# Feed-forwards on tokens and context: output pairs as seven half-size products, the second product in six parts

## The reference

```python
def swiglu(h, w1, w2):
    a, b = jnp.split(h @ w1, 2, axis=-1)
    return (jax.nn.silu(a) * b) @ w2

def ffn_sublayer(x, m, i, g, w1, w2):
    return x + HALF_STEP * m[:, 3 * i + 2, None] * swiglu(mod_norm(x, m, i, g), w1, w2)
# in second_block, for each layer l
m = (jax.nn.silu(c) @ w_mod[l] + b_mod[l]).reshape(B, N_MOD, D_MODEL)
x = ffn_sublayer(x, m, 0, norm_g[l, 0], ffn_w_in[l, 0], ffn_w_out[l, 0])      # "a"
xc = ffn_sublayer(xc, mc, 0, norm_g[l, 0], ffn_w_in[l, 0], ffn_w_out[l, 0])
...                                                                          # mixers, attention
x = ffn_sublayer(x, m, 2, norm_g[l, 2], ffn_w_in[l, 1], ffn_w_out[l, 1])      # "b"
```

## Time and profile before

| | |
|---|---|
| median of 3 runs | 3590.39 us (3589.85 to 3597.12) |
| the profiled execution | 3599.08 us |
| its span, first to last instruction | 3597.2 us |
| TensorE matmul, weight load busy | 95%, 81% |
| VectorE, ScalarE, GpSimd busy | 52%, 32%, 8% |
| mean granted TensorE clock | 0.974 |

### The profile page before, as it was taken

One profiled execution on the slowest core, in us unless ns is written; L12 is line 12 of the kernel. 1 busy time (PEld: TensorE's weight loads), 2 busy tenths in 40 slices (PEclk: granted clock), 3 DMA queues, 4 the chain that ended last, 5 costly groups with the idle time before them and its releaser, 6 DMA issues.

```text
span 3597.2 us, 45611 instructions
## 1 busy us (share of the span) xinstructions
PE 3413.5 (95%) x18534; PEld 2913.1 (81%) x18534; DVE 1884.1 (52%) x3688; ACT 1156.6 (32%) x1892; POOL 274.7 (8%) x520
## 2 busy tenths in 40 slices
PE   6989889998999999999789999999999999889998
PEld 5788667886888888878678888888888888778886
DVE  5476668446655535465677775352222364653333
ACT  4465442324221223334432122242112243332232
POOL 0000011000111100301011110000000013100000
PEclk9999899999999999999999999999999999989999
DMA  4301236333444423523145553232222244123332
GB/s 125 91 24 42 76 119 194 97 94 101 142 124 129 126 68 120 150 79 89 36 149 158 161 163 109 81 102 64 65 65 60 76 132 107 43 65 97 93 99 76
DMA packets 383473, 358.83 MB, mean 100 GB/s; under 512 B 19632, under 2 KB 351280, under 8 KB 382880
## 3 DMA queue, kind: packets, MB, share of 16 engines
q1 hardware_dynamic: 350656, 261.76, 24.1%
q0 software_dynamic: 31168, 91.94, 8.5%
q10 hardware_dynamic: 1440, 2.22, 0.2%
HBM read 349.56 MB, written 2.10 MB: 98 GB/s over the span
## 4 chain that ended last, share of the span: by engine, by line
PE 83%; DVE 11%; ACT 4%; issue 1%; DMA 1%; ACTq 0%; DVEq 0%; POOLq 0%
PE ps L626 81%; DVE lob L1964 2%; PE ps L629 1%; DVE Tm L2076 1%; ACT hib L1324 1%; DVE Hl L2087 1%; DVE ACC L2053 1%; ACT Tm L1324 1%; ACT Hh L1324 1%; DVE sm L2665 1%; ACT L1324 0%; DVE HN L2096 0%; DVE MR L1984 0%; DVE near_P L2675 0%; DVE Hl L2085 0%
## 5 line engine op out<-in xcount | busy, mean ns | idle before, releaser
L626 PE MATMUL ps<-Hh,hib 128*128 128x512 f32 (+1 forms) x3584 | 1271.0, 355 | 29.8 <-DVE lob L1964 13.4
L626 PE MATMUL ps<-Hl,hib 128*128 128x512 f32 (+1 forms) x3584 | 1260.7, 352 | 0.0
L626 PE MATMUL ps<-Hh,lob 128*128 128x512 f32 (+1 forms) x3584 | 1258.3, 351 | 0.0
L1964 DVE TENSOR_TENSOR lob<-rawb,hib 128x1024 fp32r<-128x1024 f32 (+2 forms) x499 | 597.4, 1200 | 983.6 <-ACT hib L1324 982.9
L1324 ACT ACTIVATE hib<-rawb 128x1024 fp32r<-128x1024 f32 (+2 forms) x499 | 513.6, 1033 | 1156.6 <-PE ps L626 1135.6
L626 PEld LDWEIGHTS ps<-Hh,hib 128*128 128x128 f32 x3584 | 685.1, 191 | 138.3 <-DVE lob L1964 15.3
L626 PEld LDWEIGHTS ps<-Hh,lob 128*128 128x128 f32 x3584 | 685.1, 191 | 90.1
L626 PEld LDWEIGHTS ps<-Hl,hib 128*128 128x128 f32 x3584 | 686.1, 191 | 86.6 <-issue 1.2
L626 PE MATMUL ps<-Gha,hib 128*128 128x512 f32 (+1 forms) x704 | 239.7, 340 | 6.6 <-DVE lob L1964 6.5
L626 PE MATMUL ps<-Gla,hib 128*128 128x512 f32 (+1 forms) x704 | 238.1, 338 | 0.0
L626 PE MATMUL ps<-Gha,lob 128*128 128x512 f32 (+1 forms) x704 | 238.1, 338 | 0.0
(11 more groups left out here) (264 smaller groups left out, 3807.8 us busy)
## 6 DMA issues: line engine op xcount, KB each, us to landing
rawb<-in_ffn_w_in SPq DMA_DIRECT2D x352, 256.0 KB, 3.3
rawb<-in_ffn_w_out SPq DMA_DIRECT2D x88, 512.0 KB, 3.4
rawb<-in_w_in SPq DMA_DIRECT2D x74, 512.0 KB, 3.8
MRb<-in_w_mod_t POOLq DMA_DIRECT2D x144, 256.0 KB, 3.4
rawb<-in_w_ff SPq DMA_DIRECT2D x64, 512.0 KB, 3.6
MRa<-in_w_mod_t POOLq DMA_DIRECT2D x96, 256.0 KB, 3.4
rawb<-in_ffn_w_out SPq DMA_DIRECT2D x44, 384.0 KB, 3.0
rawb<-in_w_out SPq DMA_DIRECT2D x28, 512.0 KB, 3.4
```

The lines of the kernel that those rows point to most:

```text
L626: return e.matmul(out, lhsT, rhs, start=start, stop=stop)
L1964: e.tensor_tensor(lob_of(c), raw_of(c), hib_of(c), ALU.subtract).then_inc(*done(("lo", c.i)))
```

## The change

In a0, b0 and a1 the parts of the feed-forward are 2, 4, 4, 4, 4 and 4 output pairs instead of 11 and 11 (b1 stays as it is). The first two pairs of a stage are computed as before; the other 20 by Strassen's scheme: the weights of a pair are a 2 x 2 matrix of blocks (even and odd k-tiles; gate and value columns), the activations one too (even and odd k-tiles; tokens 0 to 383 and 384 to 767), and seven products of sums of blocks take the place of eight. A product (`seven`) is 4 k-tiles x 3 matmuls of 384 columns into a PSUM bank of its own.

- GpSimd makes the five sums of weight blocks of each pair (`weights_sums`: two in place in `rawb`, three in `SUM2`), a step of 128 x 512 each. ScalarE and VectorE make high and low halves of all seven as units of 512 columns; `hib` and `lob` become a ring of six such units.
- The sums of activation blocks are made once a stage, 20 steps of 384 columns of each kind, in groups beside the two plain pairs and the first part's sweep: VectorE adds the high halves and subtracts the rounded sum, ScalarE rounds, GpSimd adds the low halves, and GpSimd (12) or VectorE (8) adds both rests.
- ScalarE copies three of the seven products out of PSUM, VectorE combines them in eight adds, then silu, multiply, high and low half on 384 columns, twice.
- The rows of `w_mod`: 48, 96, 48 and 96 in the first block, a0, b0 and a1. ScalarE's queue issues their loads in place of GpSimd's, at its next step, when VectorE has used a slot. In a crossed pair two rows are made (b0: one), in a chunk of the sweeps of parts 1 to 4 three (b0: two); what is left is made before the last sweep.

```diff
+ORDER = [1, 7, 6, 5, 3, 4, 2]
+ACTS = {1: (1, 1, 4), 7: (2, -1, 4), 6: (3, -1, 1), 5: (1, 1, 2), 2: (3, 1, 4), 3: (1,), 4: (4,)}
+WEIGHTS = {1: (1, 1, 4), 7: (3, 1, 4), 6: (1, 1, 2), 3: (2, -1, 4), 4: (3, -1, 1), 5: (4,), 2: (1,)}
+SUMS = [(m, q) for m in (1, 7, 6, 5, 2) for q in range(4)]
+SUMS_BY = (4, 4, 4, 2, 2, 2, 2)
+PLAIN = 2
+HALF = 384
+TURNS = {("a", 0): 1, ("b", 0): 2, ("a", 1): 3}
+def parts_of(j, l):
+    sizes = (PLAIN, 4, 4, 4, 4, 4) if crossed(j, l) else (11, 11)
...
-        mod_turns = [(0, 0, 48, 2), (0, 48, 96, 2), (1, 0, 144, 3)]
+        mod_turns = [(0, 0, 48, 2, 0), (0, 48, 96, 3, 2), (1, 0, 48, 2, 1), (1, 48, 96, 3, 2)]
...
# TensorE
+            def seven(N, name):
+                for x in P[name].units:
+                    b, before = take("o", name, x.m)
+                    w.wait_ge(*at("lo", x.u))
+                    freed(before)
+                    for q in range(4):
+                        if len(ACTS[x.m]) == 3:
+                            w.wait_ge(*at("e", N, x.m, q))
+                        wh, wl = (half_of(buffer, x)[:, 128 * q:128 * q + 128] for buffer in (hib, lob))
+                        mm(ps[:, b, 0:HALF], wh, acts_sum(N, 0, x.m, q), q == 0, False)
+                        mm(ps[:, b, 0:HALF], wh, acts_sum(N, 1, x.m, q), False, False)
+                        m = mm(ps[:, b, 0:HALF], wl, acts_sum(N, 0, x.m, q), False, q == 3)
+                    m.then_inc(*done(("full", name, x.m), ("used", x.u)))
...
-                    ga = {s: (Gh, Gl, OFF[s][0], OFF[s][1], (lambda k, s=s: ("g", (j, l), part_, s, k)), False) for s in sets}
+                    ga = {s: (Gh, Gl, OFF[s][0], OFF[s][1], (lambda k: ("g", N, part_, k)), False) for s in sets}
...
# ScalarE
+            def mod_more():
+                while mod["owed"] and mod["at"] < many:
+                    w.wait_ge(*at("modused", turn, u - 3 if u >= 3 else None))
+                    e.dma_start(mod_slots[turn][m], ...)
...
+                for pos, x in enumerate(P[name].units):
+                    mod_more()
+                    high_halves(reach(u=x.u))
+                    run_later()
+                    if mod["turn"] is not None and pos in (2, 4) and pos // 2 <= mod_turns[mod["turn"]][4]:
+                        mod_used(1)
+                    if pos == 6:
+                        gate("a1")
+                        high("a1", 0)
+                        gate("a2")
+                        high("a2", 1)
+                    elif x.m in copied:
+                        copy(copied[x.m], x.m)
...
# VectorE
+                for pos, x in enumerate(P[name].units):
+                    low_halves(reach(u=x.u))
+                    run_later()
+                    if m == 1:
+                        tmp("seven", name, "b2")
+                    elif m == 7:
+                        w.wait_ge(*at("copied", name, "b2"))
+                        add("a1", slot("b2"), product(7), ALU.add, ("free", "o", name, 7))
+                    elif m == 6:
+                        add("b2", slot("b2"), product(6), ALU.add, ("free", "o", name, 6))
+                    elif m == 5:
+                        w.wait_ge(*at("copied", name, "b1"))
+                        own()
+                        add("a1", slot("a1"), slot("b1"), ALU.subtract)
+                    elif m == 3:
+                        own()
+                        add("b1", slot("b1"), product(3), ALU.add)
+                        add("b2", slot("b2"), product(3), ALU.add, ("free", "o", name, 3))
+                    elif m == 4:
+                        w.wait_ge(*at("copied", name, "a2"))
+                        own()
+                        add("a1", slot("a1"), slot("a2"), ALU.add, ("whole", name, "a1"))
+                    else:
+                        gated("a1", "b1")
+                        add("a2", slot("a2"), product(2), ALU.add, ("whole", name, "a2"))
+                        add("b2", slot("b2"), product(2), ALU.subtract, ("free", "o", name, 2))
+                        low("a1", 0)
+                        own()
+                        gated("a2", "b2")
+                        low("a2", 1, ("g", N, part, f))
+                    if mod["turn"] is not None and pos in (2, 4):
+                        mod_step(1 if pos // 2 <= mod_turns[mod["turn"]][4] else 0)
...
# GpSimd
+            def weights_sums(N, name, before):
+                for c in x.chunks:
+                    w.wait_ge(*at("raw", c.i))
+                for m in (1, 7, 6, 3, 4):
+                    b1, sign, b2 = WEIGHTS[m]
+                    if m in (1, 7, 6):
+                        w.wait_ge(*at("lo", before[m] if before else None))
+                    else:
+                        own()
+                    e.tensor_tensor(weights_source(N, of[m]), weights_block(x, b1), weights_block(x, b2),
+                                    ALU.add if sign > 0 else ALU.subtract).then_inc(*done(("sum", of[m].u)))
```

More of the change, by code:

```diff
@@ new lines, in ffn @@
+                for part_, (f0, many) in enumerate(parts):
+                    for f in range(f0, f0 + many):
+                        name = (N, "in", f)
+                        if crossed(*N) and f >= PLAIN:
+                            seven(N, name)
+                        else:
+                            whole(name, fm_products, acts, between)
+                            between = None
+                            give_all(name)
+                            mark("pe", "plain", N)
+                    ga = {s: (Gh, Gl, OFF[s][0], OFF[s][1], (lambda k: ("g", N, part_, k)), False) for s in sets}
+                    residual((N, "out", part_), sets, ga, following(l, i) if part_ == len(parts) - 1 and len(sets) == 2 else None)
+                    mark("pe", "gfree", N, part_)
@@ L1367, in gemm @@
-            def gemm(name, ahead=AHEAD, between=None):
+                    for u in x.before:
+                        w.wait_ge(*at("used", u))
+                    if x.chunk:
+                        w.wait_ge(*at("raw", x.chunk.i))
+                        act(hib_of(x.chunk), raw_of(x.chunk), ACT.Copy).then_inc(*done(("hi", x.u)))
+                        continue
+                    if len(WEIGHTS[x.m]) == 3:
+                        w.wait_ge(*at("sum", x.u))
+                    else:
+                        for c in x.cross.chunks:
+                            w.wait_ge(*at("raw", c.i))
@@ L1370, in gemm @@
                 if between:
[L1371 removed]
+                    high_halves(reach(rest[0]))
                     steps = norm_steps(*between)
@@ new lines, in ffn @@
+            def ffn(j, l, i, sets, between):
+                N = (j, l)
+                if N in TURNS:
+                    mod.update(turn=TURNS[N], at=0, owed=3)
+                    mod_more()
+                    silu(TURNS[N])
+                Gh = G2[N][0]
+                parts = parts_of(j, l)
+                if crossed(j, l):
+                    in_turn(grouped([lambda m=m, q=q: acts_sums(N, m, q) for m, q in SUMS], SUMS_BY))
+                for part, (f0, many) in enumerate(parts):
+                    for f in range(f0, f0 + many):
+                        name = (N, "in", f)
+                        if crossed(j, l) and f >= PLAIN:
+                            seven(N, name, part, f - f0)
+                            continue
@@ new lines, in ffn @@
+            def ffn(j, l, i, sets, between):
+                N = (j, l)
+                Gh, Gl = G2[N]
+                if N in TURNS:
+                    mod_begin(TURNS[N])
+                parts = parts_of(j, l)
+                if crossed(j, l):
+                    in_turn(acts_sums(N))
+                for part, (f0, many) in enumerate(parts):
+                    last = part == len(parts) - 1
+                    for f in range(f0, f0 + many):
+                        name = (N, "in", f)
+                        if crossed(j, l) and f >= PLAIN:
+                            seven(N, name, part, f - f0)
+                            continue
+                        whole(name, between, False)
```

403 lines of the change are left out of this document (295 added, 108 removed).

## The result

The changed kernel took 3910.4 us (median of 4 runs, 3904.7 to 3912.4) beside 3592.3 us (4 runs, 3589.9 to 3597.1) for the kernel before: a ratio of 1.088, 95% interval 1.086 to 1.090. It is slower, as forecast, but by 318 us and not by 74, and it lies well above the range of 3530 to 3770 us.

What follows compares the result with a forecast made beforehand. It took TensorE's streamed columns to bound the kernel now; -124 for columns and the costs without holds summed to -30, holds added 80 and 24: +74 us, 3664 us, own range 3610 to 3700, wider range 3530 to 3770.

Steps and rivals of the forecast that it cites:

- the holds: GpSimd's sums block VectorE's two-SBUF-operand steps: 8 us a part, 80 us in a0 and a1, 24 in the stage openings.
- Columns, -124 us: Crossed pairs in a0, b0, a1: 84 products of 384 columns take 14.6 us, not 16.6; TensorE saves 124 us.
- The crossed pair with rows: VectorE's time per crossed pair, steps plus waits, without holds: 15.8 us in a0 and a1, 13.4 in b0, against TensorE's 14.6.
- The joint: Where the second product starts, TensorE waits for the last k-tile: about 2.3 us at 15 joints, 35 us.
- 4 x 15.8 + 31.3 - 0.3: A part of a0 or a1 where VectorE bounds it: four crossed pairs plus second-product sweep, 94.2 us without holds.
- Rival 1: The engines do not hold each other for two-operand steps: sum -30, 3560 us, faster; chance 0.27 for 3520 to 3583.
- 3 (all hidden): Rows and joints find slack and TensorE bounds the pairs: 3490 to 3510 us; chance 0.08.
- 4 (all cancels): Joints and openings near upper ends without the hold, or a third of it: within 7 us of today; chance 0.08.
- rival 2: Holds not covered, 14 us a part in all three stages, openings 22 a stage: 3794 us; chance 0.18 for above 3700.
- The openings: At each stage's start, activation sums delay the first seven-fold pair: 9 us a stage, plus 8 a stage for holds.
- The burst ahead of the last sweep: Eight leftover modulation rows made at once before the last sweep of a0 and a1: TensorE stalls 7 us, twice, 14 in all.
- The last sweep's norm: The last part's context sweep, hiding the next norm, falls from 31.7 to 11.5 us: 3 us a stage, 9 in all.

Runs made afterwards that it cites:

- With memsets: The changed kernel with each of GpSimd's weight sums replaced by two memsets of the same tile, writing but not reading: 3780.2 us.
- the six parts alone: The changed kernel with its six parts but every output pair computed as before, no seven products or GpSimd sums: 3648.9 us, ratio 1.0151.

## Why the prediction was right in its direction and wrong in its size

The forecast hung the direction on the holds: without them its sum was -30 us, 3560. The direction came out, but not by that alone. With memsets, where the weight sums hold nobody, the kernel takes 3780.2 us, and without the rows too 3607.9, both above the kernel before. So it would have been slower with no hold from the weight sums at all, and that the sign was right is partly luck. The size failed on the rows, and with them on the sum for a part in a0 and a1. Point by point:

1. **Columns, -124 us.** Right at the high clock. Products of 384 columns start every 0.173 us, and a part without rows and holds takes 93.8 us, against 100.5 with plain pairs in the run of the six parts alone. Without rows, reads and activation sums TensorE is busy for 119 us less than before. In the changed kernel, with the same 17814 products, it is only 18 us less: the forecast put the clock at nothing, and the last section shows what it took.
2. **VectorE's hold, 8 us a part.** Right: 8.1 in a0 and a1 (114.5 against 106.3), forecast 80 us for the ten parts. Wrong for b0: I had it hidden under 93.8 us, and a part of b0 falls from 102.7 to 95.6 when the sums don't read. By stage, a0 loses 46 us to the reading sums, b0 43 and a1 43.
3. **The crossed pair with rows, "15.8 us in a0 and a1 and 13.4 in b0".** Here the sum broke first. A pair's cycle can be read from the chain of waits after, at the three adds that end each pair (start, us):

```profile
1109.11 1.48 DVE Tm L2802 x3
...
1128.75 1.48 DVE Tm L2802 x3
...
1145.92 1.49 DVE Tm L2802 x3
```

   It is 19.64 us with a burst of GpSimd's sums and 17.17 without one; a burst costs 2.5 us, where the forecast gave 2.7 (five times 0.94 less 2.0). The terms named in the prediction were there, 1.15 us behind each row among them, and the 1.4 us by which 17.17 exceeds the forecast's 15.8 are waits. What I didn't count is that VectorE's next low half and gate steps wait again for ScalarE, which has fallen back by the row's wait (the idle times of 1.56 and 0.59 in the timeline below).
4. **The joint, "about 2.3 us", and the part, "4 x 15.8 + 31.3 - 0.3".** This is the step of the prediction that failed, and it is mostly one of form: without holds it gave 94.2 us for a part, and 106.3 were measured. I took the larger of two rates, TensorE's and VectorE's, as if a lagging VectorE worked on through the sweep. But the sweep is a gate: its k-tiles need VectorE's last step of the last pair, and the next pair's products need TensorE's end of the sweep. So VectorE's lag is paid at each joint, and the sweep's full 33.3 us comes after it. The timeline of VectorE ahead of the joint at 1128.70, with memsets, shows what is late:

```profile
1119.62 0.68 DVE L2228 CUSTOM_DVE_ANT_0 MRa<-MRa 128x512 f32<-128x512 f32 x1
1120.23 0.69 DVE L2228 CUSTOM_DVE_ANT_0 MRa<-MRa 128x512 f32<-128x512 f32 x1
1122.48 1.23 DVE L2202 TENSOR_TENSOR lob<-rawb,hib 128x1024 fp32r<-128x1024 f32 x1 [1.56 <-ACT hib L1472]
1123.81 0.56 DVE L2802 TENSOR_TENSOR Tm<-Tm 128x384 f32<-128x384 f32 x1
1124.96 0.56 DVE L2802 TENSOR_TENSOR Tm<-Tm 128x384 f32<-128x384 f32 x1 [0.59 <-ACT Tm L1472]
1125.43 1.01 DVE L2802 TENSOR_TENSOR Tm<-Tm,ps 128x384 f32<-128x384 f32 x2
1126.36 0.55 DVE L2811 TENSOR_TENSOR Gla<-Tm,Gha 128x384 fp32r<-128x384 f32 x1
...
1128.09 0.56 DVE L2811 TENSOR_TENSOR Gla<-Tm,Gha 128x384 fp32r<-128x384 f32 x1 [0.59 <-ACT Gha L1472]
```

   TensorE stands from 1120.40, all seven products and the sweep's first ones done. At that time VectorE is at the pair's second row. Behind it stand, in VectorE's order, a high half it has to wait for, a low half of 1024 columns that belongs to the sweep's later chunk, the gates and the last adds; the last line is the step that ends TensorE's wait. Without rows the joint is 1.35 us (or 2.1 to 4.2 with holds), with two rows a pair 8.3, holds or not. In b0, with one row a pair, it is 5.4 with holds and some 2.1 without, and a part takes 102.7 us on average (four periods), not 93.8. Of the 12.1 us that the sum for a part is short, four cycles at 17.17 in place of 15.8 would explain 5.5; the other 6.6 are the form.
5. **The rivals.** Rival 1 (no hold) fell with the stretched low halves, rivals 3 (all hidden) and 4 (all cancels) with the joints. The time of rival 2, the uncovered holds, was nearest (3794), but its reason held in b0 alone, where the holds cost 7.1 us a part and the rival gave 4.8. In a0 and a1, where it had most of its 234 us, the holds were no larger than forecast.
6. **The openings, 9 us a stage and 8 for holds.** Too small. Without holds and rows they are 22, and 12 of them are the wait behind the two plain pairs, which the forecast didn't name. The late start of the first seven-fold pair, which it took at some 4 us, is a wait of 5.9 to 6.8 for VectorE's updates in the changed kernel. In the changed kernel the first joint comes 181.4 us after the stage's start; without rows, reads or activation sums it comes after 130.7, of which 20.9 are the longer part: some 30 us a stage, against 17.
7. **The burst ahead of the last sweep, 7 us twice.** Right in kind, somewhat too small. It is there (sixteen of VectorE's steps from 1493.5 to 1506.1). In a0 TensorE waits 2.9 us for a low half behind it and then 5.1 for the norm's sum, for which it waits 0.9 in b0, where there is no burst. From its first product to that of the context's sweep this last sweep takes 48.4 us in a0, 46.9 in a1 and 31.3 in b0; less their joints (8.3, 8.3, 2.3) that is 11 and 10 us more than in b0, at a mean granted clock of 0.81 and 0.87 against 0.95.
8. **The last sweep's norm, 3 us a stage.** Too small. In the 75 us around the start of the context's last sweep (15 before, 60 behind) TensorE waits 6.5, 3.4 and 6.5 us in a0, b0 and a1 of the kernel before, 17.9, 22.2 and 19.0 in the changed one (in a0 and a1 with 4 us of item 7's burst in them), and 16.1, 18.8 and 15.8 in the one without rows, reads and activation sums. So in that last one the norm costs 9 us more in a0 and a1 each and 15 at the end of b0, with the silu of item 9 in it, and a lower clock behind it.
9. **The silu in a1, 5 us.** At the start of a1 TensorE's two waits for the norm take 11.3 and 7.2 us in the changed kernel, but 8.3 to 8.9 and some 5 to 7 of that are there at the ends of a0 and a1 too: little is left for the silu, some 3 us.

What this adds up to: a0's and a1's parts 10 x (114.5 - 102.2) = 123 us; b0's 5 x (102.7 - 93.8) = 45; the openings 3 x 13 = 39; that is 207 of the 244 us by which the forecast was short. The other 37 are about what the ends show: some 7 more than forecast for the two bursts (item 7), some 20 for the norms with the silu (34 against 14, items 8 and 9), and the lower clock behind them. But no run isolated them; they are read from traces, and a kernel with six parts and the old length of the last sweep wasn't tried.

As the sum should have been made: a part where VectorE lags is its own lag at the joint (8.3), plus the sweep (33.3), plus three of VectorE's cycles (51.5), plus the first pair. The last term isn't measured: 13.2 is what remains of 106.3, with the other small waits and the lower clock in it. The forecast's rate formula gave 94.2, and 12.1 x 10 is the largest error in it.

## What to carry to other kernels

Where two engines hand work back and forth through a gate (a second product that needs the last piece of the first), the time isn't the larger of their two loads: whatever lag the slower one has gathered is paid at each gate (8.3 us here, ten times), so count the steps that stand ahead of the gate's last one in its engine's order, and multiply by the number of gates. Small unrelated work that is threaded between such steps isn't free because its engine idles for a third of the time: the rows cost 252 us, nearly all of the 293 that VectorE works on them, and 72 of it went when their loads, 0.34 us each to issue, were issued where ScalarE needn't wait for the other engine. Cutting an exchange into more parts multiplies openings, joints and ends; an eighth of the columns in the crossed pairs, 124 us, didn't pay for them here in any version with the whole computation.

## What the runs showed of the hardware

GpSimd's additions with two SBUF operands stretch VectorE's steps with two SBUF operands: 0.69 us to 1.0, 1.3 and 1.8 in one burst, and take 1.50 to 1.64 themselves on average in place of 1.29; memsets of the same size stretch none of these low halves, and VectorE's steps of 384 columns with one operand in PSUM keep 0.55 beside the additions. That was expected in kind. Not expected was that the effect on the whole depends so much on who else uses the slack: 50 us or 130 for the same reads. And TensorE's granted clock falls around the joints. Four windows of the kernel after, over a joint, the sweep behind it, another joint, and the last 10 us of this third window by themselves (the granted clock is the number ahead of the last two):

```profile
1019.00:1036.00 17.00, 7.04 (x34) 5.98 (x35) 11.93 (x24) 6.14 (x10) 0.00 (x0) 0.89 0.42 124
1036.00:1069.00 33.00, 33.00 (x184) 28.71 (x185) 30.24 (x69) 3.45 (x6) 7.57 (x5) 0.96 0.43 128
...
1475.00:1500.00 25.00, 14.14 (x55) 11.35 (x54) 19.15 (x45) 6.84 (x12) 0.00 (x0) 0.80 0.39 125
1490.00:1500.00 10.00, 6.40 (x16) 5.00 (x17) 8.91 (x25) 1.51 (x3) 0.00 (x0) 0.51 0.41 131
```

It is 0.89 and 0.80 on average in the stretches in which TensorE stands, a mixture of the levels of 1.2 and 2.4 GHz, and still 0.96 in the sweep behind; 0.51, the lower level, where it starts again after the wait of 8.31 us that ends at 1493.60. The timeline shows the price there, two products of 512 columns at the lower level and two at the higher:

```profile
1495.90 0.63 PE L750 MATMUL ps<-Gha,lob 128*128 128x512 f32 x1
1496.33 0.63 PE L750 MATMUL ps<-Gha,hib 128*128 128x512 f32 x1
...
1500.45 0.40 PE L750 MATMUL ps<-Gha,lob 128*128 128x512 f32 x1
1500.68 0.40 PE L750 MATMUL ps<-Gha,hib 128*128 128x512 f32 x1
```

The first two start 0.43 us apart, the others 0.23. Thirteen products in a row are that slow behind this joint, and six behind the one of 1035.78: a stall of 8 us costs another 1.2 to 2.5 us in slow products. Counted over the whole trace, 798 products of the changed kernel start between 1.6 and 2.1 times as far apart as at the higher level and so cost 117 us more; they are 344 and 48 us in the kernel before, and 315 and 45 in the one without rows, reads and activation sums. So by this count some 70 of the changed kernel's 318 us are slow products, inside the parts, openings and ends above. The page of that last kernel, to be read beside the changed kernel's 3395.6 us for the same 17814 products, points the same way:

```profile
PE 3294.9 (93%) x17814; PEld 2900.4 (82%) x17814; DVE 2051.9 (58%) x3680; ACT 1342.7 (38%) x2351; POOL 454.3 (13%) x881
```
